# Four norms summed in pairs on VectorE, and latent attention's input split once with its gains in the weights

## The chip, the cores and the metric

The kernel is one program on one core of one Trainium2 chip. A core has five engines that run side by side, each taking its own instructions strictly in order: TensorE (PE in the profile, with its weight loads as PEld), VectorE (DVE), ScalarE (ACT), GpSimd (POOL) and SyncE (SP), which here starts nearly all transfers. They share an on-chip memory (SBUF, 128 partitions) and the banks that TensorE writes (PSUM; the array `ps` has eight of 512 float32 a partition). They wait for each other only through semaphores. The metric is the device time of one execution in microseconds (us), as the median of several runs; lower is better.

## The reference, cut to what matters

256 tokens with 1024 features go through two blocks of two layers each. The first block is a convolution layer, then multi-head latent attention, each followed by an MLP; what bears on this change is:

```
def rms_norm(x, g):
    y = xf * rsqrt(mean(xf * xf, axis=-1) + 1e-6);  return y * g

h = h + rms_norm(m, mix_post_g[layer])
f = squared_relu_mlp(rms_norm(h, ffn_pre_g[layer]), w_ff1[layer], w_ff2[layer])
h = h + rms_norm(f, ffn_post_g[layer])

# latent attention, layer 1: two inputs, the same h with two gains
hn   = rms_norm(h, kv_in_g)
c_kv = rms_norm(hn @ w_dkv, kv_norm_g)          # 1024 -> 256
k_rope = apply_rope(hn @ w_kr, cos, sin)        # 1024 -> 64
k_nope, v = c_kv @ w_uk, c_kv @ w_uv
hn   = rms_norm(h, mix_pre_g[1])
q    = rms_norm(hn @ w_dq, q_norm_g) @ w_uq     # 1024 -> 384 -> 1536
```

The second block begins with another norm of h (`attn_norm`, called attn_0) and a wide input projection.

## The kernel before, in words

Activations lie with features on the partitions and tokens along the row: h is 8 chunks of 128 features x 256 tokens. Every float32 factor is split into a high and a low float16 part, and a product of 128 features is three float16 matmuls: high x high, low x high, high x low. Weights are streamed from HBM in units of 4096 columns into two slots of `staged`; ScalarE makes `w_hi` of a half unit (2048 columns), VectorE the rest, `w_lo`. `split(g)` is half unit g on either engine, and each engine has its splits at fixed places of its program.

A norm before a product is applied late. TensorE multiplies the gained but not yet normalised h (x_hi, x_lo) by the weights, and the products are multiplied by the tokens' scale (`LATE_SCALE`, in `stat`) when VectorE takes them from PSUM. The tokens' sums of squares come from TensorE: a 128x128 matrix of ones times the 128x256 squares `sq`, in float32, accumulated over the 8 chunks in bank 7 (`STAT`). ScalarE takes the root (L1528), VectorE the reciprocal (L2271).

At four norms, ffn_pre_0, mix_pre_1 (with kv_in), ffn_pre_1 and attn_0, the products begin while h is still being made. After TensorE has spread the previous norm's scale over a row (L713), VectorE runs `post`: for each chunk it scales m (L2304); GpSimd adds m into h (L2161, chunk 0 on VectorE at L2308); ScalarE makes the high part (L1546) and the square (L1551) in `begin`; VectorE makes the low part (`low`, L2276). TensorE's `together` (L645, L646, L650) works chunk by chunk through two or three output banks at once, with one ones-matmul per chunk in `add_square` (L728).

Latent attention's input (kv_in and mix_pre_1) has two gains on the same h, so `begin` and `low` make two splits: f_hi, f_lo for the key and value side, x_hi, x_lo for the query side (L1550, L2280). TensorE does two of the three kv outputs in `together`, the third and the three dq outputs afterwards. VectorE multiplies each output by LATE_SCALE into kT or qT (L2673), ScalarE squares them, TensorE sums them (`sums`, L719), ScalarE takes a root over 256 columns, VectorE a reciprocal over 256 columns, and the scaled latents are split for the next products (`scale`, `his`). Then come the ukv products (eight key chunks with a ring of four banks, then values at L1115 to L1117) and uq.

What sets the order around the change is this handwritten program order of each engine and the semaphore waits in it; no planner is involved. `keep_warm` and `fill` (L743, L749) are matmuls on zeros while TensorE would have nothing to do.

Of the kernel before, what the change touches and what calls it, by code (L numbers as in the profile page):

```python
# [31 lines left out]
P = 128  # L32
# [66 lines left out]
USED = {2 * FIRST["kv"] + 1: 3 * D - HALF, 2 * FIRST["dq"] + 1: 3 * D - HALF, 2 * FIRST["uq"]: 5 * Q_RANK,  # L99
# [42 lines left out]
SCALED_GAINS = ("mix_pre_0", "ffn_pre_0", "mix_pre_1", "kv_in", "ffn_pre_1", "attn_0", "ffn2_0", "attn_1", "ffn2_1")  # L142
VECTORS = [*((_name, DC) for _name in SCALED_GAINS), ("mix_post_0", DC),
# [41 lines left out]

LATE = ("mix_pre_0", "ffn_pre_0", "mix_pre_1", "ffn_pre_1", "attn_0", "ffn2_0", "attn_1", "ffn2_1")
# [8 lines left out]
SCALE_AT = _starts(["kv_norm", "q_norm", "g_ckv"])  # L195

# [65 lines left out]
def conformer_mla_fox_dsa_moba_kernel(nc, w_stream, vec_dram, band_dram, const_dram, x_dram, pos_dram, out_dram):  # L262
    with ExitStack() as ctx:
# [63 lines left out]
        by_token = sb("by_token", [P, 12])  # L327

# [6 lines left out]
        STAT = ps[:, 7, 0:T]  # L335

# [19 lines left out]
        m_squared = sem("m_squared")  # L356
        m_added = sem("m_added")
# [97 lines left out]
        q_in_hi = sem("q_in_hi")  # L455
        q_in_lo = sem("q_in_lo")
# [152 lines left out]
        def _(pe):  # L609
# [112 lines left out]
            def add_square(name, c):  # L722

                if c == 0:

                    pe.wait_ge(rooted, NORM_AT[name])
                pe.wait_ge(squared, SQUARE_AT[name] + c + 1)
                last = pe.matmul(STAT, k("ones"), sq[:, c, :], start=(c == 0), stop=(c == DC - 1))  # L728
                if c == DC - 1:
                    last.then_inc(summed, 1)  # L730
# [313 lines left out]
            def mlp(layer):  # L1044
# [13 lines left out]
                add_square(f"ffn_pre_{layer}", DC - 1)  # L1058
# [22 lines left out]
            together("kv", 2, f_hi, f_lo, "mix_pre_1")  # L1081
            add_square("mix_pre_1", DC - 1)
            linear("kv", 3, f_hi, f_lo, done=2)
            u = FIRST["dq"]
            for j in range(3):
                if j != 1:
                    arrived(2 * u + j // 2)
                features(ps[:, 4 + j, 0:T], u % 2, j * D, DC, x_hi, x_lo,
                         None if j else lambda c: pe.wait_ge(q_in_lo, c + 1)).then_inc(product["dq"], 1)
                if j == 0:  # L1090
                    sums("kv_norm")
# [3 lines left out]
            pe.wait_ge(drained["kv"], 3)  # L1095
            n = 0
            for j in range(HEADS):
# [24 lines left out]
            for j in range(12):  # L1122
# [113 lines left out]
            add_square("attn_0", DC - 1)  # L1236
# [256 lines left out]
        def _(act):  # L1493
# [11 lines left out]

            def quarter(g, q):
# [14 lines left out]
            def root(name):  # L1521
# [15 lines left out]
            def begin(name, dst, ready, i, c, ahead=0, posted=None):  # L1537
# [8 lines left out]
                act.activation(dst[:, at, :], h[:, at, :], ACT.Copy,  # L1546
                               scale=vec[:, bass.ds(i * 2 + (VCOL["kv_in" if name == "mix_pre_1" else name] + c), 1)]
                               ).then_inc(x_hi_ready, 1)
                if name == "mix_pre_1":
# [290 lines left out]
            for n in range(8):  # L1840
                evac("ukv", n, kT[:, n, :])
                if n == 2:
                    root("q_norm")
# [1284 lines left out]
```

## Time and profile before

| | |
|---|---|
| median of 3 runs | 1157.59 us (1157.3 to 1158.06) |
| the profiled execution's own time | 1157.17 us |
| its span, first to last instruction | 1155.3 us |
| TensorE busy, matmuls | 1138.1 us (99%) |
| VectorE busy | 830.5 us (72%) |
| ScalarE busy | 657.6 us (57%) |
| GpSimd busy | 131.5 us (11%) |
| granted TensorE clock, mean | 0.999 |

"Busy" is the share of the span in which an instruction of the engine was running. A float16 matmul record of 256 columns is 273 ns long but the next begins 109 ns after it, since they are pipelined; a float32 matmul of 256 columns is two records. So costs on TensorE are read from start to start. The "idle before" at the end of a row is how long its engine stood still just before, and the name behind it is what ended that.

### The profile page before, as it was taken

How to read it: one execution, taken by the hardware profiler on the slowest of the kernel's cores; microseconds unless marked ns; L12 is line 12 of the kernel's file. 1: busy time of each engine (PE TensorE's matmuls, PEld its weight loads, DVE VectorE, ACT ScalarE, POOL GpSimd, SP SyncE). 2: the span in 40 equal slices, each digit the busy share in tenths (PEclk: the TensorE clock that was granted, in tenths of full speed). 3: DMA queues.
4: the chain of work that ended last, by engine and by line, in shares of the span. 5: the costliest groups of instructions: out<-in, count | busy, mean ns of one | idle time of the engine just before them, and what ended most of it. 6: DMA issues, size and time to landing. Idle time of an engine off the chain costs nothing.

```text
span 1155.3 us, 26283 instructions
## 1 busy us (share of the span) xinstructions
PE 1138.1 (99%) x10449; PEld 965.0 (84%) x10449; DVE 830.5 (72%) x1326; ACT 657.6 (57%) x1019; POOL 131.5 (11%) x168
## 2 busy tenths in 40 slices
PE   8999999999999999999999999999999999999998
PEld 7778888888778888888877688888877778888887
DVE  7787776655786786655569869786666666978664
ACT  7575666434667576433475767654455656765432
POOL 0000200000203200000243310000124531000010
PEclk9999999999999999999999999999999999999999
DMA  9752376555363366555453337554665344765451
GB/s 346 263 195 85 115 239 199 200 186 185 131 236 107 137 225 200 200 185 184 149 210 110 123 134 256 187 189 151 185 238 178 114 147 148 251 193 184 151 181 55
DMA packets 31466, 206.55 MB, mean 179 GB/s; under 512 B 3488, under 2 KB 3872, under 8 KB 10144
## 3 DMA queue, kind: packets, MB, share of 16 engines
q1 hardware_dynamic: 31104, 205.00, 52.1%
q8 instruction: 52, 0.85, 0.3%
q10 hardware_dynamic: 288, 0.52, 0.1%
q14 instruction: 22, 0.18, 0.1%
HBM read 204.46 MB, written 1.05 MB: 178 GB/s over the span
## 4 chain that ended last, share of the span: by engine, by line
PE 87%; DVE 8%; ACT 2%; issue 1%; DMA 1%; POOL 0%; SPq 0%; DVEq 0%
PE ps L619 21%; PE ps L620 20%; PE ps L621 20%; DVE w_lo L2257 2%; PE ps L974 1%; PE ps L882 1%; PE ps L1415 1%; PE ps L884 1%; PE ps L883 1%; PE ps L1417 1%; PE ps L1416 1%; PE ps L650 1%; PE ps L728 1%; PE ps L645 1%; PE ps L646 1%
## 5 line engine op out<-in xcount | busy, mean ns | idle before, releaser
L1498 ACT ACTIVATE w_hi<-staged 128x2048 f16<-128x2048 f32 (+2 forms) x195 | 344.8, 1784 | 237.6 <-PE ps L621 229.1
L619 PE MATMUL ps<-f_hi,w_hi 128*128 128x256 f16 x1596 | 435.0, 273 | 0.2 <-issue 0.2
L620 PE MATMUL ps<-f_lo,w_hi 128*128 128x256 f16 x1596 | 435.0, 273 | 0.0
L621 PE MATMUL ps<-f_hi,w_lo 128*128 128x256 f16 x1596 | 435.0, 273 | 0.0
L2257 DVE SCALAR_TENSOR_TENSOR w_lo<-staged,w_hi 128x2048 f16<-128x2048 f32 (+2 forms) x195 | 414.5, 2139 | 23.7 <-ACT w_hi L1498 23.5
L619 PE MATMUL ps<-x_hi,w_hi 128*128 128x256 f16 x696 | 189.8, 273 | 0.6 <-DVE tmp L2620 0.6
L621 PE MATMUL ps<-x_hi,w_lo 128*128 128x256 f16 x696 | 189.7, 273 | 0.0
L620 PE MATMUL ps<-x_lo,w_hi 128*128 128x256 f16 x696 | 189.7, 273 | 0.0
L620 PEld LDWEIGHTS ps<-f_lo,w_hi 128*128 128x128 f16 x1596 | 156.2, 98 | 19.3
L619 PEld LDWEIGHTS ps<-f_hi,w_hi 128*128 128x128 f16 x1596 | 156.2, 98 | 18.6 <-issue 0.4
L621 PEld LDWEIGHTS ps<-f_hi,w_lo 128*128 128x128 f16 x1596 | 156.2, 98 | 18.1
L619 PEld LDWEIGHTS ps<-x_hi,w_hi 128*128 128x128 f16 x696 | 68.0, 98 | 14.0 <-issue 4.8
L2161 POOL TENSOR_TENSOR h<-h,m 128x256 f32<-128x256 f32 x28 | 23.9, 882 | 489.6 <-DVE m L2304 489.6
L620 PEld LDWEIGHTS ps<-x_lo,w_hi 128*128 128x128 f16 x696 | 68.1, 98 | 8.2
L621 PEld LDWEIGHTS ps<-x_hi,w_lo 128*128 128x128 f16 x696 | 68.1, 98 | 7.9
L2646 DVE TENSOR_SCALAR m<-ps 128x256 f32 (+1 forms) x16 | 6.8, 425 | 63.4 <-PE ps L621 54.4
L2620 DVE SCALAR_TENSOR_TENSOR tmp<-ps,stat 128x256 f32<-128x256 f32 x64 | 26.9, 421 | 33.7 <-PE ps L621 33.7
L2006 ACT ACTIVATE tmp<-pad,vec 128x256 f32<-128x256 f32 x44 | 26.4, 600 | 38.6 <-DVE pad L2864 38.4
L2864 DVE TENSOR_TENSOR pad<-ps,stat 128x256 f32<-128x256 f32 x44 | 18.6, 424 | 32.6 <-PE ps L621 32.6
L1778 ACT ACTIVATE tmp<-tmp 128x256 f32<-128x256 f32 x64 | 26.3, 410 | 20.2 <-DVE tmp L2620 20.1
L2154 POOL TENSOR_TENSOR probs<-probs,peak 128x128 f32<-128x128 f32 x64 | 31.8, 529 | 35.0 <-DVE peak L2462 35.0
L882 PE MATMUL ps<-f_hi,w_hi 128*128 128x256 f16 x128 | 35.0, 273 | 0.0
(380 smaller groups left out, 1775.4 us busy)
## 6 DMA issues: line engine op xcount, KB each, us to landing
staged<-weights SPq DMA_DIRECT2D x165, 1024.0 KB, 5.1
staged<-weights SPq DMA_DIRECT2D x32, 704.0 KB, 4.2
xn<-bands SPq DMA_DIRECT2D x3, 512.0 KB, 9.9
m<-bands SPq DMA_DIRECT2D x3, 512.0 KB, 8.1
cst<-constants SPq DMA_DIRECT2D x1, 1027.0 KB, 7.9
h<-x_turned SPq DMA_DIRECT2D x2, 512.0 KB, 4.8
staged<-weights SPq DMA_DIRECT2D x2, 512.0 KB, 6.9
qT<-bands SPq DMA_DIRECT2D x2, 512.0 KB, 11.6
```

Source lines behind the costliest of these rows:

```text
L619: pe.matmul(out, wh, xh[:, c, :], start=(c == 0), stop=False)
L620: pe.matmul(out, wh, xl[:, c, :], start=False, stop=False)
L621: last = pe.matmul(out, wl, xh[:, c, :], start=False, stop=(c == kc - 1))
L882: pe.matmul(out, wh, f_hi[:, c, :], start=(c == 0), stop=False)
L1498: act.activation(w_hi[:, s, o:o + n], staged[:, s, o:o + n], ACT.Copy, scale=SW).then_inc(hi_split, 1)
L1778: act.activation(tmp[:, 2 + n % 2:3 + n % 2, :], r, ACT.Square)
L2006: act.activation(tmp[:, j, :], pad[:, j, 0:T], ACT.Identity, bias=vec[:, bass.ds(i * 4 + (VCOL[f"b_cv_{layer}"] + n), 1)], scale=vec[:, ba ...
L2154: last = pool.tensor_tensor(at, at, peak[:, r, 6 + t:7 + t].to_broadcast([P, P * (t + 1)]), ALU.mult)
L2161: pool.tensor_tensor(h[:, c, :], h[:, c, :], m[:, c, :], ALU.add).then_inc(h_ready[ready], 1)
L2257: dve.scalar_tensor_tensor(w_lo[:, s, o:o + n], staged[:, s, o:o + n], SW, w_hi[:, s, o:o + n], ALU.mult, ALU.subtract).then_inc(lo_split, 1)
L2620: dve.scalar_tensor_tensor(tmp[:, n % 2, :], ps[:, n % RING, 0:T], 0.0, LATE_SCALE, ALU.max, ALU.mult).then_inc(drained[one], 1)
L2864: dve.tensor_tensor(pad[:, j, TAPS2 - 1:TAPS2 - 1 + T], ps[:, j, 0:T], LATE_SCALE, ALU.mult).then_inc(drained[up], 1)
```

## The change

Three parts, in one edit.

First, at the four norms VectorE adds the squares of the chunks in pairs (`add_pair`, four float32 additions of 128x256 a norm, behind the low parts of chunks 2, 4, 6 and 7), and TensorE sums four pair sums in place of eight squares. In `together` they stand ahead of chunk 4, chunk 6 and, two of them, chunk 7.

Second, latent attention's input is split once, with the plain factor SX. The gains kv_in and mix_pre_1 go into the weights: the kv and dq units are laid out by input chunk, 384 columns each (`GAINED`), and `with_gain` on ScalarE and VectorE splits each 384 columns with that chunk's gain as scale. The gains are multiplied by SW in an instruction of their own at the program's start. TensorE works all three outputs of kv chunk by chunk, then all three of dq.

Third, its norms go by token. The sums are matmuls with the squares as stationary side and one column of ones, two for each 128x256 (`token_square`); root and reciprocal act on 128x2 or 128x4 (`latents`); `row_of` spreads a scale over a row with float32 matmuls against the identity, and ScalarE copies the row to SBUF. The latents are taken from PSUM directly, without LATE_SCALE; the epsilon is corrected for that (`eps_terms`, `variance`).

```diff
+            def add_pair(name, i):            # VectorE
+                dve.wait_ge(squared, SQUARE_AT[name] + 2 * i + 2)
+                dve.tensor_tensor(sq[:, 2 * i, :], sq[:, 2 * i, :], sq[:, 2 * i + 1, :], ALU.add).then_inc(pair_added, 1)
...
                     if c >= 2:
                         low(norm, c - 2, dst)
+                    if c in (4, 6, 8, 9):
+                        add_pair(norm, (4, 6, 8, 9).index(c))
...
                 for c in range(DC):           # TensorE, together
-                    if squares and c:
-                        add_square(norm, c - 1)
+                    for i in {4: (0,), 6: (1,), 7: (2, 3)}.get(c, ()) if squares else ():
+                        add_pair(norm, i)
...
             split(1)                          # VectorE, start of the program
+            at = slice(VCOL["kv_in"], VCOL["mix_pre_1"] + DC)
+            dve.tensor_scalar(vec[:, at], vec[:, at], SW, None, ALU.mult).then_inc(gains_scaled, 1)
+            dve.wait_ge(gains_scaled, 2)
             invert("mix_pre_0")
...
-                if name == "mix_pre_1":       # low(): the second split goes
-                    dve.wait_ge(q_in_hi, c + 1)
-                    dve.scalar_tensor_tensor(x_lo[:, c, :], h[:, c, :], v(name, c), x_hi[:, c, :], ALU.mult,
-                                             ALU.subtract).then_inc(q_in_lo, 1)
...
+            for c in range(DC):               # TensorE, kv, then dq
+                for i in {4: (0,), 6: (1,), 7: (2,)}.get(c, ()):
+                    input_pair(i)
+                pe.wait_ge(x_hi_ready, SPLIT_AT["mix_pre_1"] + c + 1)
+                with_gain("kv", 0, c)
+            input_pair(DC // 2 - 1)
+            for c in range(DC):
+                with_gain("dq", 4, c)
+                if c == 1:
+                    pe.wait_ge(rooted, NORM_AT["kv_norm"])
+                    pe.wait_ge(eps_terms, len(LATENT))
+                    latent_sums("kv_norm")
+                if c == 4:
+
+                    pe.wait_ge(inverted, NORM_AT["kv_norm"] + 1)
+                    row_of(12, 0)
+                    row_of(10, T).then_inc(latent_rows, 1)
...
+            with_gain("dq", range(DC))        # VectorE, in place of splits, reciprocals and latent()
+            dve.wait_ge(rooted, NORM_AT["mix_pre_1"] + 1)
...
+            variance("kv_norm", 8)
+            dve.wait_ge(rooted, NORM_AT["kv_norm"] + 1)
+            dve.reciprocal(latents[:, 10:14], latents[:, 0:4]).then_inc(inverted, 2)
+            split(2 * FIRST["kv"] + 4)
+            scale("kv_norm", 0, (f_hi[:, 8:10], f_lo[:, 8:10]))
...
+            variance("q_norm", 14)
             split(2 * FIRST["dq"] + 4)
-            invert("q_norm")
-            scale("q_norm", qT, "q_norm", (f_hi[:, 10:13], f_lo[:, 10:13]))
+            dve.wait_ge(rooted, NORM_AT["q_norm"] + 1)
+            dve.reciprocal(latents[:, 18:20], latents[:, 16:18]).then_inc(inverted, 1)
+            scale("q_norm", 4, (f_hi[:, 10:13], f_lo[:, 10:13]))
```

Where the instructions stand. On VectorE in `post` ahead of ffn_pre_0, from the m scaling of chunk 4 on, before:

```order
L2304 SCALAR_TENSOR_TENSOR m<-m,vec,ps 128x256
L2276 SCALAR_TENSOR_TENSOR x_lo<-h,vec,x_hi 128x256
L2304 SCALAR_TENSOR_TENSOR m<-m,vec,ps 128x256
L2276 SCALAR_TENSOR_TENSOR x_lo<-h,vec,x_hi 128x256 x3
L2257 SCALAR_TENSOR_TENSOR w_lo<-staged,w_hi 128x2048
L2271 RECIPROCAL stat<-stat 128x256
```

and in the changed kernel, from the low part of chunk 2 on (L2413 is the addition of a pair, L2402 the low part, L2431 the scaling of m):

```order
L2402 SCALAR_TENSOR_TENSOR x_lo<-h,vec,x_hi 128x256
L2413 TENSOR_TENSOR sq<-sq 128x256
L2431 SCALAR_TENSOR_TENSOR m<-m,vec,ps 128x256
L2402 SCALAR_TENSOR_TENSOR x_lo<-h,vec,x_hi 128x256
L2431 SCALAR_TENSOR_TENSOR m<-m,vec,ps 128x256
L2402 SCALAR_TENSOR_TENSOR x_lo<-h,vec,x_hi 128x256
L2413 TENSOR_TENSOR sq<-sq 128x256
L2431 SCALAR_TENSOR_TENSOR m<-m,vec,ps 128x256
L2402 SCALAR_TENSOR_TENSOR x_lo<-h,vec,x_hi 128x256 x2
L2413 TENSOR_TENSOR sq<-sq 128x256
L2402 SCALAR_TENSOR_TENSOR x_lo<-h,vec,x_hi 128x256
L2413 TENSOR_TENSOR sq<-sq 128x256
```

Each addition stands directly behind a low part, the first two of them ahead of the scaling of a later m, which GpSimd waits for.

On VectorE between the last low parts of latent attention's input and the split of ukv's first half, before:

```order
L2257 SCALAR_TENSOR_TENSOR w_lo<-staged,w_hi 128x2048
L2271 RECIPROCAL stat<-stat 128x256
L2673 TENSOR_TENSOR kT<-ps,stat 128x256
L2257 SCALAR_TENSOR_TENSOR w_lo<-staged,w_hi 128x1024
L2673 TENSOR_TENSOR kT<-ps,stat 128x256
L2257 SCALAR_TENSOR_TENSOR w_lo<-staged,w_hi 128x2048
```

and in the changed kernel:

```order
L2386 SCALAR_TENSOR_TENSOR w_lo<-staged,vec,w_hi 128x384 x8
L2805 TENSOR_SCALAR latents<-ps 128x2 x2
L2813 TENSOR_TENSOR latents<-ps,latents 128x2
L2818 RECIPROCAL latents<-latents 128x4
L2371 SCALAR_TENSOR_TENSOR w_lo<-staged,w_hi 128x2048
L2421 SCALAR_TENSOR_TENSOR xn<-ps,vec,stat 128x256 x2
L2407 SCALAR_TENSOR_TENSOR f_lo<-xn,f_hi 128x256 x2
```

The 256-column reciprocal and the takings into kT are gone; eight splits with gains and five small instructions stand ahead of ukv's first half.

On TensorE at the end of kv in the changed kernel (L1112, L1113 and L1118 are the products with gained weights, L1125 the one-column sums), chunk 7, the last pair and the beginning of dq:

```order
L1112 MATMUL ps<-f_hi,w_hi 128x256
L1113 MATMUL ps<-f_hi,w_lo 128x256
L1118 MATMUL ps<-f_lo,w_hi 128x256 x3
L1125 MATMUL ps<-cst,sq 128x1 x2
L1112 MATMUL ps<-f_hi,w_hi 128x256
```

Before, this place had a ones-matmul of 256 columns and then the 24 products of kv's third output.

## Rows read from the trace of the kernel before

**Rows 1.** The page: busy time of each engine over the whole span.
```profile
PE 1138.1 (99%) x10449; PEld 965.0 (84%) x10449; DVE 830.5 (72%) x1326; ACT 657.6 (57%) x1019; POOL 131.5 (11%) x168
```

**Rows 2.** TensorE's waits, whole span, two of them: who for whom, us, times, longest.
```profile
PE ps L650 <- DVE f_lo L2276: 2.2, 6, 0.4
...
PE ps L619 <- DVE tmp L2620: 0.6, 2, 0.3
```

**Rows 3.** The chain of waits at attn_0: start us, us, what.
```profile
570.07 0.43 PE ps L728 x2
```

**Rows 4.** TensorE in order of time at attn_0: start us, us, instruction.
```profile
567.30 0.27 PE L645 MATMUL ps<-x_hi,w_hi 128*128 128x256 f16 x1
567.41 0.27 PE L646 MATMUL ps<-x_hi,w_lo 128*128 128x256 f16 x1
...
568.15 0.50 PE L650 MATMUL ps<-x_lo,w_hi 128*128 128x256 f16 x3
```

**Rows 5.** VectorE in order of time at attn_0: chunk 0, chunk 3's low part, chunk 7's.
```profile
566.19 0.42 DVE L2308 TENSOR_TENSOR h<-h,m 128x256 f32<-128x256 f32 x1
566.53 0.86 DVE L2304 SCALAR_TENSOR_TENSOR m<-m,vec,ps 128x256 f32<-128x256 f32 x2
...
570.15 0.56 DVE L2276 SCALAR_TENSOR_TENSOR x_lo<-h,vec,x_hi 128x256 f16<-128x256 f32 x1
570.63 0.47 DVE L2304 SCALAR_TENSOR_TENSOR m<-m,vec,ps 128x256 f32<-128x256 f32 x1
...
573.61 0.48 DVE L2276 SCALAR_TENSOR_TENSOR x_lo<-h,vec,x_hi 128x256 f16<-128x256 f32 x1 [0.29 <-ACT x_hi L1546]
```

**Rows 6.** VectorE at latent attention's input, second chunk and last.
```profile
299.00 0.47 DVE L2276 SCALAR_TENSOR_TENSOR f_lo<-h,vec,f_hi 128x256 f16<-128x256 f32 x1
299.40 0.95 DVE L2280 SCALAR_TENSOR_TENSOR x_lo<-h,vec,x_hi 128x256 f16<-128x256 f32 x1
...
308.08 0.47 DVE L2280 SCALAR_TENSOR_TENSOR x_lo<-h,vec,x_hi 128x256 f16<-128x256 f32 x1
308.47 2.28 DVE L2257 SCALAR_TENSOR_TENSOR w_lo<-staged,w_hi 128x2048 f16<-128x2048 f32 x1
310.67 1.74 DVE L2271 RECIPROCAL stat<-stat 128x256 f32<-128x256 f32 x1
```

**Rows 7.** GpSimd over the same stretch.
```profile
299.16 0.90 POOL L2161 TENSOR_TENSOR h<-h,m 128x256 f32<-128x256 f32 x1 [0.75 <-DVE m L2304]
```

**Rows 8.** TensorE, latent attention: first kv product, first low part, last value products.
```profile
297.03 0.27 PE L645 MATMUL ps<-f_hi,w_hi 128*128 128x256 f16 x1
...
297.88 0.39 PE L650 MATMUL ps<-f_lo,w_hi 128*128 128x256 f16 x2 [0.26 <-DVE f_lo L2276]
...
332.65 0.38 PE L1116 MATMUL ps<-w_lo,f_hi 128*128 128x512 f16 x1
332.87 0.38 PE L1117 MATMUL ps<-w_hi,f_lo 128*128 128x512 f16 x1
```

**Rows 9.** Busy by stretch: us, then PE, PEld, DVE, ACT, POOL, clock, DMA share, GB/s.
```profile
297.00:309.20 12.20, 9.98 (x66) 6.59 (x66) 12.20 (x23) 9.90 (x24) 5.92 (x7) 1.00 0.01 1
1146.00:1155.00 9.00, 3.67 (x32) 3.13 (x30) 2.78 (x6) 1.95 (x4) 0.00 (x0) 0.86 0.31 117
```

**Rows 10.** TensorE at 89 and 1147 us: one-column sums, transposes of 128 columns.
```profile
89.52 0.61 PE L1021 MATMUL ps<-cst,xn 128*128 128x1 f32 x4
89.98 0.58 PE L1021 MATMUL ps<-cst,sq 128*128 128x1 f32 x4
...
1147.07 1.07 PE L1470 MATMUL ps<-cst,m 128*128 128x128 f32 x8
```

**Rows 11.** The chain of waits at the program's start.
```profile
15.25 1.82 DVE w_lo L2257
...
17.46 1.76 DVE stat L2271
...
23.52 1.42 DVE kT L2525 x2
```

More of the change, by code:

```diff
@@ L195 @@
 SCALE_AT = _starts(["kv_norm", "q_norm", "g_ckv"])
+PAIRED = ("ffn_pre_0", "mix_pre_1", "ffn_pre_1", "attn_0")
+PAIRS_AT = {_name: DC // 2 * _i for _i, _name in enumerate(PAIRED)}
 SQUARE_AT = _starts(["mix_pre_0", "ffn_pre_0", "mix_pre_1", "kv_norm", "q_norm", "ffn_pre_1", "attn_0", "g_ckv", "ffn2_0",
@@ L1080, in _, with with_gain @@
             pe.wait_ge(late_loaded, 48)
[L1081 to L1091, printed above, removed]
+            def with_gain(name, first, c):
+                u = FIRST[name]
+                if c % (DC // 2) == 0:
+                    arrived(2 * u + c // (DC // 2))
+                o = gained_columns(c).start
+                for j in range(3):
+                    wh, wl = weights(u % 2, o + P * j, P)
+                    pe.matmul(ps[:, first + j, 0:T], wh, f_hi[:, c, :], start=(c == 0), stop=False)
+                    pe.matmul(ps[:, first + j, 0:T], wl, f_hi[:, c, :], start=False, stop=False)
+                if name == "kv":
+                    pe.wait_ge(x_lo_ready, SPLIT_AT["mix_pre_1"] + c + 1)
+                for j in range(3):
+                    wh, wl = weights(u % 2, o + P * j, P)
+                    last = pe.matmul(ps[:, first + j, 0:T], wh, f_lo[:, c, :], start=False, stop=(c == DC - 1))
+                    if c == DC - 1:
+                        last.then_inc(product[name], 1)
@@ new lines, in token_square, with input_pair @@
+            def token_square(i, src, start, stop):
+                for t in range(TT):
+                    last = pe.matmul(ps[:, 7, TT * i + t:TT * i + t + 1], src[:, P * t:P * t + P], k("ones", 1), start=start and t == 0,
+                                     stop=stop and t == TT - 1)
+                return last
+            def input_pair(i):
+                if i == 0:
+                    pe.wait_ge(rooted, NORM_AT["mix_pre_1"])
+                pe.wait_ge(pair_added, PAIRS_AT["mix_pre_1"] + i + 1)
+                last = token_square(0, sq[:, 2 * i, :], i == 0, i == DC // 2 - 1)
+                if i == DC // 2 - 1:
+                    last.then_inc(summed, 1)
@@ new lines, in latent_sums, with row_of @@
+            def latent_sums(name):
+                n = NORM_CHUNKS[name]
+                for c in range(n):
+                    pe.wait_ge(squared, SQUARE_AT[name] + c + 1)
+                    last = token_square(1 + LATENT.index(name), sq[:, c, :], c == 0, c == n - 1)
+                last.then_inc(summed, 1)
+            def row_of(at, first):
+                for t in range(TT):
+                    last = pe.matmul(ps[:, 7, first + P * t:first + P * t + P], latents[:, at + t:at + t + 1].to_broadcast([P, P]),
+                                     k("ident"), start=True, stop=True)
+                return last
@@ L1802, in mlp @@
                     unit(i, 1)
[L1803 removed]
+                if layer == 0:
+                    act.wait_ge(gains_scaled, 2)
+                    act.wait_ge(product[two], units - 1)
+                    with_gain("kv", range(DC))
+                else:
+                    unit(units // 2 - 1, 0)
                 last_square(product[two], DC, ps[:, 1, 0:T], INVF)
@@ L3027, in stream_of @@
     kr = a["kv_w_kr"]
-    put("kv", 0, 0, columns(np.concatenate([a["kv_w_dkv"], kr, kr], axis=1)))
-    put("dq", 0, 0, columns(a["mla_w_dq"][0]))
+    for name, w in (("kv", np.concatenate([a["kv_w_dkv"], kr, kr], axis=1)), ("dq", a["mla_w_dq"][0])):
+        w = whole(w)
+        for e in range(2):
+            put(name, 0, HALF * e, [w[:, GAINED * DC // 2 * e:GAINED * DC // 2 * (e + 1)]])
     put("ukv", 0, 0, columns(a["kv_w_uk"]))
```

182 lines of the change are left out of this document (112 added, 70 removed).

## The prediction

> **What bounds the kernel now.** I read the page first: TensorE's matmuls fill 99% of the span, VectorE 72% and ScalarE 57% [rows 1]. So what takes time off TensorE's own queue shortens the whole, unless TensorE then waits. The table of TensorE's waits comes next: the reader is to see that a few waits lie just where the change is, 2.2 us in six waits for f_lo at latent attention's input and 0.6 us in two behind ffn_pre_0 and ffn_pre_1 [rows 2]. Then the chain of waits, for the price of one ones-matmul, 0.43 us [rows 3]. Last the order of time of TensorE, VectorE and GpSimd at attn_0 and at latent attention, for the paces that meet there [rows 4 to 8], and the stretches for the clock [rows 9].
>
> **Paces.** From start to start a float16 matmul of 256 columns takes 0.11 us (0.109 over longer runs) [rows 4], one of 512 columns 0.22 [rows 8]. VectorE's plain float32 addition takes 0.34 from its start to the next one's, a scaling of m 0.39 (two in 0.86, the last one 0.47 long) [rows 5]. Between a low part and the next scaling of m lie 0.48 [rows 5], so one chunk costs VectorE 0.87. In `together` with three banks one chunk is 9 matmuls, 0.98 us, plus before one ones-matmul of 0.43, together 1.41: TensorE had 0.5 us of slack a chunk. Now it has 0.1.
>
> **The pairs at ffn_pre_0, ffn_pre_1 and attn_0.** Each loses four of eight ones-matmuls: 12 x 0.43 = 5.2 us off TensorE's queue.
>
> The additions do not come free. An addition has two inputs in SBUF, as the low part has. In latent attention the second of two low parts in a row takes 0.95 us where the last one takes 0.47, and GpSimd's addition into h begins between them and lasts 0.90 [rows 6, 7]. So VectorE stood about 0.47 for GpSimd. The pair addition is in that very position, directly behind a low part while GpSimd works: I price it at 0.34 + 0.47 = 0.81 us for the first two; the last two come when GpSimd is nearly done, 0.34 each. The Trainium skill has a rule for it (SBUF — State Buffer, "SBUF: two separate sides"): a VectorE instruction with two SBUF inputs and a GpSimd instruction exclude each other, whoever is first keeps the shared ports for its whole instruction. By the rule the price could be larger than the row's; that is the second rival.
>
> Now attn_0 step by step. TensorE gets the first low part at 568.15 [rows 4]; with 0.98 a chunk it asks for chunk 3's at 571.09. Before, that low part was there at 570.15 + 0.56 = 570.71 [rows 5]; with the first addition ahead of it, at 571.52. That is a wait of 0.4. Chunk 4 and the pair's matmul give TensorE 0.98 + 0.43, VectorE needs 0.87; at chunk 5, behind the second addition, the wait is 0.1 or so. The pairs 2 and 3, asked for ahead of chunk 7, are then done: VectorE's last low part began at 573.61 [rows 5], plus some 1.3 for additions, plus 0.7 for the last two gives 575.7; TensorE asks at 567.30 + 8.8 = 576.1. So each of the three norms gains 1.7 - 0.5 = 1.2 us, 3.6 in all. Behind ffn_pre_0 and ffn_pre_1 the sum is now complete one chunk before the products, so root and reciprocal (1.74 us, rows 6) are done in time and the 0.6 us of waits [rows 2] go. Sum 4.2. Bounds: without any block or wait 5.8; with every addition at 0.81 and pair 3 late as well, 0.9 less a norm, 1.5.
>
> **Latent attention, kv to the last value product.** Before: from 297.03 to 332.87 + 0.22 [rows 8], 36.1 us. In it are 192 float16 matmuls of 256 columns (144 for kv and dq, 48 for the keys), 20.9; 24 of 512, 5.2; and 14 float32 ones (8 + 2 + 3 sums and one rotation) at 0.43, 6.0. Together 32.1, so TensorE stood 4.0 us: nearly all in the first stretch, where VectorE was busy 12.20 of 12.20 us [rows 9], with two low parts of 0.40 + 0.87 and a scaling of m per chunk.
>
> After: the float16 work is the same (8 chunks x 9 x 2). The sums become 4 + 2 + 3 = 9 pairs of one-column matmuls. Two of these take 89.98 - 89.52 = 0.46 us [rows 10]: one column is no cheaper than 256, 9 x 0.46 = 4.1. The Trainium skill (TensorE: Matmul & The Clock Gate, "Wait — 56ns, not 53.3ns?") has starts at least 25 ns apart however few the columns; by that the nine would cost under 1 us and the sum would be 3 us better. The row, with float32 weights loaded for each, decides against it. The rows of scales are 6 float32 matmuls of 128 columns, eight records in 1.07 us [rows 10], so 0.23 each, 1.4. The rotation moves behind uq's first product and stays 0.43. Work 32.0: nothing is gained in TensorE's work here, all of it must come from the 4.0 us of waits.
>
> What is late next? One low part per chunk puts VectorE at attn_0's pace. Chunk 0's low part costs 0.1 to 0.2 as there [rows 4], the first addition 0.2 at chunk 3 (its low part has a plain factor, slightly shorter). Then dq's weights: attn_0 and this stage are alike with 270.27 us between them (567.30 to 297.03, rows 4 and 8), so VectorE's last low part, 573.61 there, comes near 304.7 here with the additions, the last addition ends 305.4. Then VectorE makes four low splits of 384 columns before dq's first half counts. 2048 columns took 2.20 (308.47 to 310.67, rows 6), 256 take 0.39; 384 I put at 0.52, so 307.5. TensorE has kv and the last pair done at 297.88 + 0.33 + 7 x 0.98 + 0.3 + 4 x 0.46 = 307.2 and waits 0.3 to 0.4. The second half of dq takes VectorE until 309.6, then the two epsilon terms, 309.9; TensorE asks for them at 309.5, wait 0.4. Waits in all 1.2, so 33.2 us instead of 36.1: a gain of 2.9.
>
> The rest of the chain I cost at nothing, by these covers. The kv scale (sum, root, reciprocal of a few columns) has three chunks of dq, 2.9 us, ahead of it. ukv's first products wait for VectorE's low parts of the latents, due 0.5 us before. The q scale has five key products (3.3 us) over it; in VectorE's queue the split of uq's first half, some 2.1 us, stands ahead of its reciprocal, which leaves a few tenths only. If that cover is gone, up to 2 us are exposed there. The ScalarE side loses eight high parts and trades half splits for 384-column ones; it has idle time. SP's transfers keep their order, and dq's low splits end earlier than before, so uq's load does too. Bounds: 4.1 with no wait at all, 0.9 with the q chain uncovered.
>
> **Start of the program.** The added scaling of 16 columns and its wait stand on VectorE between w_lo and the reciprocal, and the chain of waits runs through just these [rows 11]. A column operation with its own wait: I take 0.2 us lost, bounds 0 and 0.4.
>
> **Sum.** 4.2 + 2.9 - 0.2 = 6.9 us. The profiled execution took 1157.17 us, so 1150.3; the median of the runs lies 0.42 above it, so I forecast 1150.7 us.
>
> **Rivals.**
> 1. *The additions cost TensorE nothing.* For it: the block is seen only where POOL's addition started first. Against: the addition is in the same place as the long x_lo. It gives 1.6 us more at the norms, 0.3 at latent attention, and one or two tenths: 1148.7.
> 2. *The additions block for a whole GpSimd instruction.* By the rows, 0.90 [rows 7] in place of 0.47: chunk 3 waits 0.8, chunk 5 0.6, so 0.9 more for each of four norms, 3.6: 1154.3. That is how the rule of the Trainium skill on the shared ports (SBUF — State Buffer) would have it at its worst. Against: the row shows half.
> 3. *The small instructions of the latent norms are exposed.* Sum, variance, root, reciprocal, row, copy, scaling and split go round five times between TensorE, VectorE and ScalarE, behind splits of 2.2 us in their queues. The latent stage gains 0.9 only: 1152.7.
> 4. *Slower: the clock falls.* If TensorE stands several us at the q scale, the granted clock may fall to its lower level, as in the last 9 us, where it was busy 3.67 and the mean granted clock was 0.86 [rows 9]. At half the clock the 32 us of latent work at 0.109 go to 0.218 for as long as it lasts; with 12 us of work at the lower level the stage costs 12 more and the whole comes out at 1163. It decides from some 7 us of work at the lower level. Against: between 297 and 309.2 TensorE was busy only 9.98 of 12.20 us and the clock stayed 1.00 [rows 9].
> 5. *Nothing to gain.* TensorE is not what bounds the stretches behind these norms and the gain is waited away: 1156 to 1157. Against it: the waits of TensorE are a few us in all.
>
> **Chances.** Forecast 0.62 (own range 1149.4 to 1152.0), rival 1 0.12, rival 2 0.08, rival 3 0.11, rival 4 0.03, rival 5 0.04. From no change a measurement of this kernel can tell about 0.2%, 2.3 us: faster is below 1155.3. Faster 0.92, same 0.05, slower 0.03. The range for 8 in 10 goes from rival 1's end to rival 2's near side: 1148.5 to 1153.8.
>
> **What would show it.** TensorE's sums at L751 in the three norms: four a norm, and one wait of about 0.4 us for the low part of chunk 3. The first two additions near 0.9 us long, the last two near 0.42. In latent attention: waits for w_lo and for the epsilon terms of about 0.4 each, none for the q scale; from the first kv product to the last value product 33.2 us. One-column pairs at 0.46. I am wrong if the additions are all 0.42 long (rival 1), if waits for `latents` or `stat` of over 1 us show (rival 3), or if the granted clock leaves 1.00 there.

## The result, and the profile after

The changed kernel takes 1150.63 us (median of four runs, 1150.47 to 1150.78), the kernel before 1157.73 in the same series (1157.3 to 1158.06): a ratio of 0.9938, 95% interval 0.9926 to 0.995, so 7.1 us or 0.6% faster. The forecast was 1150.7 us. The profiled execution took 1150.78 us, the one of before 1157.17.

The page of the changed kernel: the span, and busy time of each engine.

```profile
span 1148.9 us, 26306 instructions
PE 1133.4 (99%) x10447; PEld 963.1 (84%) x10447; DVE 829.4 (72%) x1345; ACT 654.8 (57%) x1026; POOL 130.8 (11%) x168
```

TensorE still fills its span, with 4.7 us less work than in [rows 1]. VectorE has 19 instructions more and is busy 1 us less: sixteen additions and sixteen splits of 384 columns came; eight low parts, four larger splits, three reciprocals of 256 columns and six takings into kT and qT went; the rest is small work. TensorE's waits of the changed kernel (who for whom, us, times, longest):

```profile
PE ps L673 <- DVE x_lo L2402: 0.8, 3, 0.3
PE ps L1112 <- DVE w_lo L2386: 0.6, 1, 0.6
...
PE ps L1118 <- DVE f_lo L2402: 0.2, 1, 0.2
```

Against [rows 2]: the six waits of 2.2 us for f_lo have become one of 0.2, and the two for tmp no longer reach the list (they have shrunk, not gone, as the part on the prediction shows). New are three for x_lo, one in each norm with additions, and one for the weights of dq.

Where the time went is seen by cutting the span at five fixed events. Four of them are VectorE's first scaling of m of each post norm, which waits for TensorE's row of scales; first of before, then of the changed kernel; start us, us, instruction, idle before:

```profile
119.43 0.48 DVE L2304 SCALAR_TENSOR_TENSOR m<-m,vec,ps 128x256 f32<-128x256 f32 x1 [0.88 <-PE ps L713]
295.40 0.48 DVE L2304 SCALAR_TENSOR_TENSOR m<-m,vec,ps 128x256 f32<-128x256 f32 x1 [0.80 <-PE ps L713]
389.70 0.48 DVE L2304 SCALAR_TENSOR_TENSOR m<-m,vec,ps 128x256 f32<-128x256 f32 x1 [0.80 <-PE ps L713]
565.68 0.48 DVE L2304 SCALAR_TENSOR_TENSOR m<-m,vec,ps 128x256 f32<-128x256 f32 x1 [0.80 <-PE ps L713]
```

```profile
120.16 0.48 DVE L2431 SCALAR_TENSOR_TENSOR m<-m,vec,ps 128x256 f32<-128x256 f32 x1 [0.88 <-PE ps L736]
294.70 0.48 DVE L2431 SCALAR_TENSOR_TENSOR m<-m,vec,ps 128x256 f32<-128x256 f32 x1 [0.80 <-PE ps L736]
386.22 0.48 DVE L2431 SCALAR_TENSOR_TENSOR m<-m,vec,ps 128x256 f32<-128x256 f32 x1 [0.80 <-PE ps L736]
560.76 0.48 DVE L2431 SCALAR_TENSOR_TENSOR m<-m,vec,ps 128x256 f32<-128x256 f32 x1 [0.80 <-PE ps L736]
```

The fifth is TensorE's last value product of latent attention, at 332.87 in [rows 8], and in the changed kernel:

```profile
328.96 0.38 PE L1198 MATMUL ps<-w_hi,f_lo 128*128 128x512 f16 x1
```

The stretches between them, in us, for all kernels of this study (the experiments are told below). A norm with early products follows each of the four scalings: ffn_pre_0, latent attention's input, ffn_pre_1 and attn_0, so the stretches marked (A) hold one of the three norms each and (B) holds latent attention.

| kernel | start to mix_post_0 | to ffn_post_0 (A) | to last value product (B) | to mix_post_1 | to ffn_post_1 (A) | to the end (A) | from mix_post_0 on | median of runs |
|---|---|---|---|---|---|---|---|---|
| before | 119.43 | 175.97 | 37.47 | 56.83 | 175.98 | 589.62 | 1035.87 | 1157.4 to 1157.73 |
| changed | 120.16 | 174.54 | 34.26 | 57.26 | 174.54 | 588.14 | 1028.74 | 1150.63 |
| pairs_on_before | 119.47 | 174.53 | 37.48 | 56.83 | 174.53 | 588.16 | 1031.53 | 1153.52 |
| eight_at_three | 120.17 | 175.97 | 34.26 | 57.27 | 175.97 | 589.56 | 1033.03 | 1155.25 |
| eight_at_latent | 119.81 | 174.53 | 34.08 | 57.26 | 174.54 | 588.08 | 1028.49 | 1150.25 |
| sums_twice | 120.18 | 174.54 | 37.04 | 57.26 | 174.53 | 588.15 | 1031.52 | 1153.48 |
| low_twice | 119.89 | 174.52 | 37.99 | 57.27 | 174.53 | 588.10 | 1032.41 | 1154.58 |
| gains_later | 120.57 | 174.75 | 34.24 | 57.28 | 174.54 | 588.12 | 1028.93 | 1150.76 |
| pool_column | 120.36 | 173.65 | 32.53 | 57.28 | 173.58 | 587.30 | 1024.34 | 1146.53 |
| adds_last | 119.48 | 173.79 | 33.38 | 57.27 | 173.78 | 587.60 | 1025.82 | 1147.96 |
| three_changes | 120.23 | 173.79 | 34.07 | 57.26 | 173.79 | 587.56 | 1026.47 | 1148.29 |
| eps_early | 120.30 | 173.79 | 32.99 | 57.27 | 173.79 | 587.56 | 1025.40 | 1147.53 |

A stretch that an edit doesn't touch repeats within 0.02 us or so (0.08 in the long last one), far closer than the runs behind a median, which lie up to 1.2 us apart (2.4 in sums_twice). The reader can take from the first two rows: 1.43, 1.44 and 1.48 us at the three norms (A), 3.21 at latent attention (B), 0.43 given back where the rotation of the rope key now stands behind uq's first product. Together 7.13, against 7.1 in the medians. The 0.73 us at the start are nearly all scatter; 0.1 to 0.2 of such a start belong to the change (gains_later, below).

### The profile page after: what moved, and what is told of

It reads as the page before. It is cut to its first block, busy times and chain, and to the rows that moved or that the text cites. A ratio compares the mean times of both kernels' runs of the same rounds, so it can differ in the third digit from the quotient of the medians.

```text
span 1148.9 us, 26306 instructions
## 1 busy us (share of the span) xinstructions
PE 1133.4 (99%) x10447; PEld 963.1 (84%) x10447; DVE 829.4 (72%) x1345; ACT 654.8 (57%) x1026; POOL 130.8 (11%) x168
## 4 chain that ended last, share of the span: by engine, by line
PE 88%; DVE 9%; ACT 1%; issue 1%; DVEq 0%
PE ps L642 21%; PE ps L644 21%; PE ps L643 20%; DVE w_lo L2371 1%; PE ps L997 1%; PE ps L905 1%; PE ps L906 1%; PE ps L907 1%; PE ps L1497 1%; PE ps L1499 1%; PE ps L1498 1%; DVE m L2431 1%; PE ps L865 1%; PE ps L893 1%; PE ps L881 1%
## 5 line engine op out<-in xcount | busy, mean ns | idle before, releaser
L1580 ACT ACTIVATE w_hi<-staged 128x2048 f16<-128x2048 f32 (+3 forms) x191 | 338.1, 1786 | 230.6 <-PE ps L644 222.0
L2371 DVE SCALAR_TENSOR_TENSOR w_lo<-staged,w_hi 128x2048 f16<-128x2048 f32 (+3 forms) x191 | 406.7, 2141 | 27.0 <-ACT w_hi L1580 26.7
L642 PE MATMUL ps<-x_hi,w_hi 128*128 128x256 f16 x672 | 183.3, 273 | 0.0
L644 PE MATMUL ps<-x_hi,w_lo 128*128 128x256 f16 x672 | 183.2, 273 | 0.0
L643 PE MATMUL ps<-x_lo,w_hi 128*128 128x256 f16 x672 | 183.2, 273 | 0.0
L642 PEld LDWEIGHTS ps<-x_hi,w_hi 128*128 128x128 f16 x672 | 65.7, 98 | 13.1 <-issue 4.3
L644 PEld LDWEIGHTS ps<-x_hi,w_lo 128*128 128x128 f16 x672 | 65.8, 98 | 7.6
L643 PEld LDWEIGHTS ps<-x_lo,w_hi 128*128 128x128 f16 x672 | 65.8, 98 | 7.5
## 6 DMA issues: line engine op xcount, KB each, us to landing
xn<-bands SPq DMA_DIRECT2D x3, 512.0 KB, 10.1
```

Source lines behind the costliest of these rows:

```text
L642: pe.matmul(out, wh, xh[:, c, :], start=(c == 0), stop=False)
L643: pe.matmul(out, wh, xl[:, c, :], start=False, stop=False)
L644: last = pe.matmul(out, wl, xh[:, c, :], start=False, stop=(c == kc - 1))
L1580: act.activation(w_hi[:, s, o:o + n], staged[:, s, o:o + n], ACT.Copy, scale=SW).then_inc(hi_split, 1)
L2371: dve.scalar_tensor_tensor(w_lo[:, s, o:o + n], staged[:, s, o:o + n], SW, w_hi[:, s, o:o + n], ALU.mult, ALU.subtract).then_inc(lo_split, 1)
```

## The experiments

**Pairs alone, and without them.** Two kernels split the change: the kernel before with pairs at ffn_pre_0, ffn_pre_1 and attn_0, and the changed kernel with eight sums at these (code shortened).

```
 # pairs_on_before: together(), TensorE; eight_at_three is the changed kernel with the reverse
+for i in {4: (0,), 6: (1,), 7: (2, 3)}.get(c, ()) if norm in PAIRED: add_pair(norm, i)
-if squares and c: add_square(norm, c - 1)
 # post(), VectorE
+if norm in PAIRED and c in (4, 6, 8, 9): add_pair(...)
```

Expected of pairs_on_before:

> The kernel before with the pairs alone, at ffn_pre_0, ffn_pre_1 and attn_0; latent attention as before. My theory: 4.2 us faster than before, 1153.5, so that 2.9 are left for latent attention and start together. Additions that cost nothing: 1151.9. Additions that cost their whole length: 1156.2. If the two parts of the change are independent, this gain and the one that eight_at_three gives up are the same within 0.3 us; if VectorE's additions at one place delay work elsewhere, they differ.

Expected of eight_at_three:

> The changed kernel with the pairs taken back at ffn_pre_0, ffn_pre_1 and attn_0: eight ones-matmuls a norm and no additions there; latent attention keeps the changed form. My theory (four ones-matmuls of 0.43 us less a norm, but the first two additions, 0.94 us each in the changed kernel's trace, let TensorE wait 0.3 to 0.5 us at chunks 3 and 5): it is slower than the changed kernel by 4.2 us, 1154.8. If the additions cost TensorE nothing: by 5.8, 1156.4. If they cost it as much as they last: by 1.5, 1152.1.

Measured: 1153.52 us (ratio to before 0.9964, 0.995 to 0.9978) and 1155.25 (0.9977, 0.9968 to 0.9986). In the stretches the pairs bring 1.44 + 1.45 + 1.46 = 4.35 us on the kernel before, and taking them back costs 1.43 + 1.43 + 1.42 = 4.28 on the changed one. The medians alone, 4.2 and 4.6, would not tell as much. So the two parts are independent, and the pairs are worth 4.3 us against 4.2 forecast. Additions that cost nothing (5.8) and additions that cost their length (1.5) are both out.

**What makes the additions long.** First VectorE's and TensorE's rows of the changed kernel at attn_0, then GpSimd's.

```profile
564.36 0.56 DVE L2402 SCALAR_TENSOR_TENSOR x_lo<-h,vec,x_hi 128x256 f16<-128x256 f32 x1
564.84 0.94 DVE L2413 TENSOR_TENSOR sq<-sq 128x256 f32<-128x256 f32 x1
565.71 0.47 DVE L2431 SCALAR_TENSOR_TENSOR m<-m,vec,ps 128x256 f32<-128x256 f32 x1
...
569.89 0.41 DVE L2413 TENSOR_TENSOR sq<-sq 128x256 f32<-128x256 f32 x1
```

```profile
565.21 0.49 PE L673 MATMUL ps<-x_lo,w_hi 128*128 128x256 f16 x3
566.63 0.50 PE L673 MATMUL ps<-x_lo,w_hi 128*128 128x256 f16 x3 [0.28 <-DVE x_lo L2402]
566.97 0.60 PE L751 MATMUL ps<-sq,cst 128*128 128x256 f32 x2
```

```profile
562.17 3.34 POOL L2275 TENSOR_TENSOR h<-h,m 128x256 f32<-128x256 f32 x4 [167.02 <-DVE m L2431]
566.26 1.77 POOL L2275 TENSOR_TENSOR h<-h,m 128x256 f32<-128x256 f32 x2 [0.75 <-DVE m L2431]
```

The addition at 564.84 lasts 0.94 us, and GpSimd's run of four ends at 562.17 + 3.34 = 565.51, 0.27 before it. Then GpSimd stands 0.75 us, since VectorE comes to the next scaling of m so late. TensorE's low parts start 0.98 apart where nothing is late; from 565.21 to 566.63 it is 1.42, so it lost 0.44, of which the bracket shows 0.28 as idle. To test the cause, GpSimd's work was cut to one column, with all semaphores kept; this kernel leaves most of h without the addition:

```
-pool.tensor_tensor(h[:, c, :], h[:, c, :], m[:, c, :], ALU.add)
+pool.tensor_tensor(h[:, c, 0:1], h[:, c, 0:1], m[:, c, 0:1], ALU.add)
```

> The changed kernel with GpSimd's additions into h at the four posts cut to one column each (the rest of h is left without them), everything else the same. It tests the cause of the 0.94 us directly. My theory: all sixteen pair additions last 0.41, the low parts beside them 0.41 too, and TensorE's waits at chunks 3 and 5 go, with part of the wait for dq's w_lo: 2.3 us faster than the changed kernel, 1148.3. Rival (the additions are long for another reason, as their wait for ScalarE's squares): the first two stay above 0.8 us, 1150.6.

Measured: 1146.53 us (0.9904, 0.9889 to 0.9919), 4.1 us faster than the changed kernel, where 2.3 were forecast. The row of all sixteen additions, by shape (busy us, mean ns | idle before), in the changed kernel and then here:

```profile
L2413 DVE TENSOR_TENSOR sq<-sq 128x256 f32<-128x256 f32 x16 | 10.9, 680 | 0.0
```

```profile
L2413 DVE TENSOR_TENSOR sq<-sq 128x256 f32<-128x256 f32 x16 | 6.7, 421 | 0.0
```

All are 0.42 long. So GpSimd's additions are what stretched them, by 0.52 each in the eight that were long; that is shown, not only argued. The gain is larger than forecast because the low parts shorten as well (x_lo 0.48 in place of 0.56) and h is there sooner: the first low part no longer waits. At ffn_pre_0 the gain of 0.89 us is, by TensorE's starts, 0.44 + 0.11 behind the two additions, 0.14 at the first low part and 0.17 at tmp (shown in the part on the prediction).

**The additions elsewhere.** No work is taken away here; VectorE makes all four additions behind its last scaling of m, and TensorE sums them ahead of chunk 7 (at latent attention three there and the fourth behind it).

```
 # TensorE
-for i in {4: (0,), 6: (1,), 7: (2, 3)}.get(c, ()): add_pair(norm, i)
+for i in {7: (0, 1, 2, 3)}.get(c, ()): add_pair(norm, i)
 # VectorE, post()
-if c in (4, 6, 8, 9): add_pair(norm, (4, 6, 8, 9).index(c))
+for i in {8: (0, 1), 9: (2, 3)}.get(c, ()): add_pair(norm, i)
```

> The changed kernel with VectorE's four pair additions of each of the four norms behind its last scaling of m, where GpSimd's additions into h are nearly through, and TensorE's four sums ahead of chunk 7. My theory (the first two additions last 0.94 us because they stand for GpSimd, and only they make TensorE wait): additions of 0.41, no wait at chunks 3 and 5. From TensorE's own starts in the changed kernel those waits are 0.44 + 0.12 us at attn_0 and 0.40 + 0.14 at latent attention, and 0.69 for dq's w_lo; 1.7 us at the three norms and some 0.8 at latent attention go, and up to 0.2 a norm comes back ahead of chunk 7: 1.9 us faster than the changed kernel, 1148.7. Rival (the place does not matter, VectorE's total work does): 1150.6.

Measured: 1147.96 us (0.9917, 0.9904 to 0.9931), 2.7 us faster than the changed kernel. At attn_0 VectorE's last low parts and its additions, and TensorE:

```profile
564.77 0.58 DVE L2402 SCALAR_TENSOR_TENSOR x_lo<-h,vec,x_hi 128x256 f16<-128x256 f32 x1 [0.29 <-ACT x_hi L1644]
565.27 0.75 DVE L2413 TENSOR_TENSOR sq<-sq 128x256 f32<-128x256 f32 x2
565.94 0.47 DVE L2402 SCALAR_TENSOR_TENSOR x_lo<-h,vec,x_hi 128x256 f16<-128x256 f32 x1
566.34 0.75 DVE L2413 TENSOR_TENSOR sq<-sq 128x256 f32<-128x256 f32 x2
```

```profile
565.10 0.49 PE L673 MATMUL ps<-x_lo,w_hi 128*128 128x256 f16 x3
566.09 0.49 PE L673 MATMUL ps<-x_lo,w_hi 128*128 128x256 f16 x3
566.41 1.89 PE L751 MATMUL ps<-sq,cst 128*128 128x256 f32 x8
568.80 0.49 PE L673 MATMUL ps<-x_lo,w_hi 128*128 128x256 f16 x3
```

Two additions in 0.75 us, TensorE's low parts 0.98 apart, and nothing waits ahead of chunk 7: 566.41 to 568.80 are four sums and six products, 4 x 0.43 + 6 x 0.11 = 2.38, with no gap. The place decides, not VectorE's total. The gain is 0.75, 0.76 and 0.54 us at the three norms and 0.88 in B. At attn_0 that is just the 0.44 + 0.12 of chunks 3 and 5. The further 0.2 at ffn_pre_0 and ffn_pre_1 are a rest of the wait for tmp, 0.17 by TensorE's starts, which the changed kernel still has and this one hasn't (rows in the part on the prediction).

**Pairs at latent attention.** The changed kernel with eight pairs of one-column matmuls and no additions there:

```
-for i in {4: (0,), 6: (1,), 7: (2,)}.get(c, ()): input_pair(i)   # shortened
+if c: input_pair(c - 1)          # waits for ScalarE's square of the chunk, sums sq[:, i]
```

> The changed kernel with eight pairs of one-column matmuls for the sum of latent attention's input norm and no additions on VectorE there. Four pairs more on TensorE are 4 x 0.46 = 1.84 us. My theory: VectorE's additions (0.95, 0.94, 0.41, 0.41 us) are what makes TensorE wait there (0.22 for f_lo at chunk 3, about 0.15 at chunk 5, 0.56 for dq's w_lo, 0.16 for the epsilon terms), so these 1.1 us go: 0.75 us slower than the changed kernel, 1151.4. Rival: the waits come from ScalarE's and GpSimd's side and stay: 1.8 us slower, 1152.5.

Measured: 1150.25 us (0.9938, 0.9924 to 0.9951), 34.08 us in B against 34.26. Neither theory's size is right: four sums more cost less than nothing. Two rows of TensorE show why:

```profile
298.50 0.50 PE L1125 MATMUL ps<-cst,sq 128*128 128x1 f32 x4
298.87 0.27 PE L1112 MATMUL ps<-f_hi,w_hi 128*128 128x256 f16 x1
```

A pair alone between float16 products takes 0.37 us from its start to the next product's, not 0.46: four are 1.5. The waits that go are larger than I took them: by TensorE's starts 0.40 at chunk 3, 0.14 at chunk 5, 0.69 for dq's w_lo, 0.34 for the epsilon terms, 1.6 together. So at this norm, with its additions in that place, the pairs brought nothing.

**The price of a sum.** Each pair of one-column matmuls twice, which doubles the three sums:

```
+for again in range(2):
     for t in range(TT): last = pe.matmul(ps[:, 7, TT*i+t:TT*i+t+1], src[:, P*t:P*t+P], k("ones", 1), ...)
```

> The changed kernel with each of the nine pairs of one-column float32 matmuls in latent attention (4 + 2 + 3) issued twice, which doubles the three sums. At 0.46 us a pair TensorE has 4.1 us more work; four of the nine pairs stand ahead of waits of 1.1 us in all, which they take up, so 3.1 us slower, 1153.7. If a one-column matmul cost TensorE only a start 25 ns after the last (the Trainium skill, TensorE: Matmul & The Clock Gate, on the shortest distance of two matmuls), nine pairs were 0.45 us, all of it under the waits: no change, 1150.6.

Measured: 1153.48 us (0.997, 0.9959 to 0.998), B 2.78 us longer. One column is dear: back to back the second pair adds 0.45 (the row of four records lasts 0.50, of eight 0.95, of twelve 1.40), so nine are 4.05, of which the waits took 1.3. The rule of the Trainium skill (TensorE: Matmul & The Clock Gate, "Wait — 56ns, not 53.3ns?"), starts 25 ns apart at the least, is a floor that these float32 matmuls stay far above: a pair, four records, takes 0.45 us here.

**The low part that went.** In latent attention a second low part per chunk was put back, into a tile that nothing reads:

```
 # low(), VectorE, only for latent attention's input
+dve.scalar_tensor_tensor(x_lo[:, c, :], h[:, c, :], SX, dst[0][:, c, :], ALU.mult, ALU.subtract)
```

> The changed kernel with a second low part per chunk of latent attention's input, written to a tile that nothing reads there, as long as the one that the change took away; everything else as changed. My theory: the gain at latent attention came from VectorE, which was full there (12.17 of 12.17 us before, a second low part of 0.40 to 0.87 a chunk), and not from TensorE's work. VectorE's last low part comes some 8 x 0.7 = 5.6 us later, TensorE has no other work to put there, so the stage is 5 us longer, more than the whole gain of 2.8: 1155.6. Rival (the sums by tokens and the smaller norm chains brought it): at most 1 us longer, 1151.6.

Measured: 1154.58 us (0.9973, 0.9962 to 0.9984), B 37.99 us: 3.73 longer, more than the whole 3.21 that the change gained there. VectorE in this kernel, and TensorE's waits in it at latent attention:

```profile
298.01 0.41 DVE L2403 SCALAR_TENSOR_TENSOR x_lo<-h,f_hi 128x256 f16<-128x256 f32 x1
298.35 0.94 DVE L2404 SCALAR_TENSOR_TENSOR f_lo<-h,f_hi 128x256 f16<-128x256 f32 x1
...
300.80 0.41 DVE L2415 TENSOR_TENSOR sq<-sq 128x256 f32<-128x256 f32 x1
```

```profile
PE ps L1118 <- DVE f_lo L2404: 3.4, 5, 1.0
```

The waits of [rows 2] are back. I had forecast 5 us; the low part that stands for GpSimd is 0.94 now, but the addition behind it is then 0.41: in this kernel VectorE is held up for long once for each addition of GpSimd's, whichever instruction stands there.

**The start.** The scaling of the 16 gains moved from the start into the first feed-forward:

```
 # VectorE: from behind split(1), ahead of invert("mix_pre_0"), to the head of mlp(0)
 dve.tensor_scalar(vec[:, at], vec[:, at], SW, None, ALU.mult).then_inc(gains_scaled, 1)
```

> The changed kernel with the scaling of the 16 columns of gains moved from the start, ahead of the reciprocal, to VectorE's work of the first feed-forward. My theory: 0.2 us of the start come back, 1150.4. Rival 1: it costs nothing where it is, since in the changed kernel's trace it ends (17.58 + 0.17) ahead of ScalarE's root that the reciprocal waits for: 1150.6. Rival 2: the 0.7 us by which VectorE's first scaling of m is later in that trace (120.16 to 119.43) are its doing: 1149.9.

Measured: 1150.76 us (0.9941, 0.9927 to 0.9954), no difference from the changed kernel. VectorE at the start, changed kernel first, then this one:

```profile
17.58 0.17 DVE L2647 TENSOR_SCALAR vec<-vec 128x16 f32<-128x16 f32 x1
18.18 1.75 DVE L2397 RECIPROCAL stat<-stat 128x256 f32<-128x256 f32 x1 [0.43 <-ACT stat L1625]
```

```profile
18.57 1.75 DVE L2397 RECIPROCAL stat<-stat 128x256 f32<-128x256 f32 x1 [1.00 <-ACT stat L1625]
```

In these two the reciprocal waits for ScalarE's root, so the scaling seems to cost nothing. The other executions say otherwise. In adds_last the same instructions are:

```profile
17.30 0.17 DVE L2647 TENSOR_SCALAR vec<-vec 128x16 f32<-128x16 f32 x1
17.50 1.75 DVE L2397 RECIPROCAL stat<-stat 128x256 f32<-128x256 f32 x1
```

Here the reciprocal stands directly behind the scaling, and it does so in four of the eight executions with the scaling at the start (adds_last, low_twice, eight_at_latent, eps_early): there it costs 0.15 to 0.20 us, by where the root ended. In the other four the root ends last; the reciprocal then starts 0.57 us after the root's start, against 0.50 in gains_later and three_changes, 0.07 more with the scaling; why is open. In all twelve executions the first scaling of m comes 101.96 to 102.00 us behind this reciprocal, so what it loses the kernel loses.

Which of the two comes last is scatter. TensorE's first recorded product came at 11.50 us in before's execution and between 11.71 and 13.04 in the others, with the scaling or without, and the root starts 5.02 or 5.03 behind it. That scatter is nearly all of the 0.73 us in the table's first column. So neither my 0.2 nor rival 1's nothing holds in every execution, and rival 2 is out: gains_later itself has the latest start. The medians cannot tell, for a second reason too: in its new place the scaling stands ahead of a split and the reciprocal of ffn_pre_0, and TensorE waits 0.38 us for tmp there in place of 0.17. That is the stretch of 174.75 in the table.

**Both together, and one step more.** The best places known so far, three_changes joining additions last at the three norms, eight sums at latent attention and the gains later; and eps_early, which is adds_last with

```
-with_gain("dq", range(DC)); ...the two epsilon terms
+with_gain("dq", range(6)); ...the two epsilon terms; with_gain("dq", range(6, DC))
```

Expected of three_changes:

> Additions behind the last scaling at ffn_pre_0, ffn_pre_1 and attn_0; eight pairs of one-column matmuls and no additions at latent attention's input norm; the scaling of the 16 gains later. Theory: 1.7 - 0.4 us at the three norms, 0.4 from the eight sums, 0.1 from the gains, 1148.8. If additions behind the last scaling gain at latent attention too, adds_last is as fast or faster; if latent attention does better without them, this one is.

Expected of eps_early:

> adds_last with VectorE's two epsilon terms ahead of the last two of dq's eight low splits instead of behind them. In the trace of adds_last TensorE starts the kv latent's sums at 307.07 where its own pace would have it 0.3 us earlier, and the terms are made at 306.75 + 0.21. Theory: 0.3 us faster than adds_last, 1147.7, which is near what a measurement can tell, and the wait before these sums is gone in the trace. Rival: the second half of dq's weights is then late instead, no change.

Measured: 1148.29 us (0.992, 0.9906 to 0.9933) and 1147.53 (0.9911, 0.9898 to 0.9925). With the additions out of GpSimd's way pairs do pay at latent attention: B is 33.38 in adds_last and 34.07 with eight sums. The epsilon terms give 0.39 us in B, TensorE starts the kv latent's sums with no wait. eps_early is the fastest kernel of the study that does the whole work, 10.1 us faster than before and 3.1 faster than the change.

## Why the prediction was right, point by point

**The three norms, 4.2 forecast, 4.35 measured.** 5.2 us of sums went; the first two additions last 0.94 and cost TensorE 0.44 at chunk 3 and 0.12 at chunk 5 (forecast 0.4 and 0.1), the last two 0.41. The rest was off in two small terms. The wait for tmp behind ffn_pre_0 and ffn_pre_1, forecast to go, is shorter but there. At ffn_pre_0, before and then changed:

```profile
135.11 0.27 PE L621 MATMUL ps<-x_hi,w_lo 128*128 128x256 f16 x1
135.66 0.27 PE L619 MATMUL ps<-x_hi,w_hi 128*128 128x256 f16 x1 [0.28 <-DVE tmp L2620]
```

```profile
134.68 0.27 PE L644 MATMUL ps<-x_hi,w_lo 128*128 128x256 f16 x1
134.96 0.27 PE L642 MATMUL ps<-x_hi,w_hi 128*128 128x256 f16 x1
```

With 0.11 from start to start where nothing waits, 0.44 us have become 0.17: the reciprocal no longer waits for the root, but VectorE's split of 2048 columns now stands directly ahead of it. At attn_0 1.2 were forecast and 1.48 came: TensorE's wait for m in the attention behind it fell from 0.39 to 0.13 by its starts, which I had not forecast; in eight_at_three it is 0.39 again.

**Latent attention, 2.9 forecast, 3.21 - 0.43 = 2.78 measured.** From the first kv product (296.23) to the end of the last value product (328.96 + 0.22) are 32.95 us, with the rotation 33.38; 33.2 were forecast. (The remaining 0.1 of the gain lies ahead of the first product, which follows VectorE's scaling of m by 1.53 us in place of 1.63.) That the size is right is in part luck, since two terms were off in opposite directions. Work: I priced nine pairs at 0.46 each, 4.1; four single ones at 0.37, a double and a triple (to the next product 0.82 and 1.26) make 3.6. So TensorE's own work fell by 0.5, where I had written that nothing is gained in it. Waits: forecast 1.2, measured by TensorE's starts 0.30 + 0.40 + 0.14 + 0.69 + 0.34 = 1.9. The mis-sized term among them is the wait for dq's weights, forecast 0.3 to 0.4:

```profile
306.01 0.51 PE L1125 MATMUL ps<-cst,sq 128*128 128x1 f32 x4
307.07 0.28 PE L1112 MATMUL ps<-f_hi,w_hi 128*128 128x256 f16 x1 [0.56 <-DVE w_lo L2386]
```

Counted from the first kv product, TensorE was free after 306.01 + 0.37 - 296.23 = 10.15 us, just the forecast's 307.2 - 297.03 = 10.17: what four cheaper sums saved (0.36), the low parts of chunks 0, 3 and 5 took back (0.84 waited, 0.5 forecast). It was VectorE that came late. Its last addition ended 8.57 us after that product in place of 8.4, and dq's first product started after 10.84 in place of 10.5, behind four of the eight splits that take 4.33. The two errors still hang together: had the sums cost 0.46, TensorE would have come here some 0.3 later and waited that much less (an estimate from these rows).

The main claim was that all of this gain is waits that VectorE's second low part had caused. low_twice bears out the mechanism: with that low part back, more than the whole gain is gone. But all of it these waits were not: 0.5 is TensorE's own work, and its waits fell from 4.0 to 1.9.

**No wait at the q scale** was forecast and none is there; rival 3 (1152.7) is out.

**The start, 0.2 forecast, 0.07 to 0.20 measured.** The chain ran through both neighbours [rows 11], and where it still does the scaling costs up to the 0.20 that I took. In the changed kernel's own execution ScalarE's root came later than both, and 0.07 was lost. The medians show neither.

**Rivals.** Rival 1 is out (additions of 0.94), rival 2 also: TensorE lost 0.56 us a norm, not 1.4. How the rule of the Trainium skill on the shared ports reads here (SBUF — State Buffer, "SBUF: two separate sides": whichever of the two starts first holds the pair for its whole instruction): the trace agrees in kind, since VectorE's addition ends 0.27 after GpSimd's; what it pays is less than the rest of an instruction already begun (565.51 - 564.84 = 0.67), 0.52 on the average of the eight, not the 0.84 that one lasts. The clock stayed at its upper level, 2.4 GHz; windows of the latent stage, before and then changed (us, then PE, PEld, DVE, ACT, POOL, clock, DMA share, GB/s):

```profile
297.03:309.20 12.17, 9.95 (x66) 6.56 (x66) 12.17 (x23) 9.88 (x24) 5.88 (x7) 1.00 0.01 1
```

```profile
296.23:308.43 12.20, 11.29 (x102) 9.57 (x102) 12.19 (x25) 9.38 (x25) 5.78 (x7) 1.00 0.07 10
308.43:320.43 12.00, 11.84 (x110) 10.72 (x108) 7.79 (x15) 6.90 (x11) 0.00 (x0) 1.00 0.69 255
```

TensorE has 1.34 us more work in the first 12 us, VectorE is still full there and has 4 us free in the next.

## What to carry to other kernels

Work taken off a full engine comes back less what the engine that takes it over holds up. Price the new instruction in its place: a VectorE addition with both inputs in SBUF cost 0.41 us behind GpSimd's work and 0.94 beside it, and moving it a few rows, at no other cost, was worth 2.7 us of 1150. And cut both traces at the same few events: stretches repeat within 0.02 us where single runs scatter by 1, so that terms of 0.2 us can be told apart. Then look at more than one execution: what costs nothing in one (the scaling at the start) was on the path in the next.

## What the hardware showed that I had not expected

- VectorE and GpSimd hold each other up in turn: behind an addition of 0.94 GpSimd stands 0.75 us for the next m, where in adds_last it makes its seven additions in one run:

```profile
559.11 5.95 POOL L2275 TENSOR_TENSOR h<-h,m 128x256 f32<-128x256 f32 x7 [167.84 <-DVE m L2431]
```

- Of the VectorE instructions with two inputs in SBUF between two scalings of m, GpSimd held up only one for long (0.94), however many there were: in low_twice, from the second chunk on, the other low part and the addition last 0.41. In the changed kernel the low part ahead of a long addition is held a little as well, 0.56 where pool_column has 0.48.
- A pair of one-column float32 matmuls costs TensorE 0.37 us alone between float16 products and 0.45 behind another such pair.
